# The first w2 of the second expert layer kept outside the ring

## The chip, the cores and the metric

The kernel runs on one core of one Trainium2 chip. The metric is the device time of one execution in microseconds (us). The kernel before took 1134.48 us, the median of three runs (1131.81 to 1135.38). Everything is float32.

## The reference

Two layers work on 256 tokens of width 1024. Layer 0 mixes tokens by causal pooling, layer 1 by differential attention. After each mixer comes a hierarchical mixture of experts: a router gives each token two of 32 experts, and each expert has three matrices of 2 MB.

```python
def hier_moe(h, wg, bg, we, be, w1, w3, w2):
    ...
    def expert_block(args):
        xb, e = args
        a = jax.nn.silu(xb @ w1[e]) * (xb @ w3[e])
        return a @ w2[e]
    ...

def reference(...):
    for i in range(DEPTH):
        ...                                  # i = 0: pool_mixer, i = 1: diff_attention
        h = rms_norm(x, norm_ffn_g[i])
        x = x + hier_moe(h, moe_wg[i], moe_bg[i], moe_we[i], moe_be[i],
                         moe_w1[i], moe_w3[i], moe_w2[i])
    return rms_norm(x, final_g)
```

## The kernel before

All weights stream through `ring`, eight slots of 2 MB (16 KB in each of 128 partitions). The kernel walks all 32 experts of a layer in order, whichever tokens they got. In what follows the matrices of layer 1 are counted c = 0, 1, 2, ... in the order w1, w3, w2 of expert 0, then of expert 1, and so on (c = 95 is the last). Matrix c goes to slot c % 8. Experts are named e0 to e31.

SyncE alone issues the weight loads, in program order, and each load is preceded by a wait for what last read its slot. For layer 1 it issues c0 and c1 when attention is done with wv (`s_vp`), c2 to c5 when all queries and keys are computed (`s_q`, NH), and c6 and c7 when the output projection is done (`s_wo`). From c8 on, the function `stream` waits for the products that used the slot: a w1 or w3 slot is free when the gate products of its expert are done (`m_gu`), a w2 slot when its down products are done (`m_y`). So c8 and c9 wait for the gate products of e0, c10 for the down products of e0, c11 and c12 for the gate products of e1, c13 for the down products of e1.

TensorE does for each expert: gate and up products from the two ring slots (L457, function `expert`), one part of the gathering of the next group's tokens (L411), then, when VectorE has turned the activations (L1069, `actT`), the down products (L493). Both product steps do one block of 32 tokens, and a second block under `pe.If(count > SB)` only where the expert has more than 32 tokens. After four experts (a group) TensorE adds the outputs back to the tokens (L510, `scatter`, here too one or two blocks by a branch). `keep_clock` (L363) adds products that nobody reads. Eight experts are the body of a loop of four iterations. VectorE and ScalarE copy each expert's output (L1095, L799) into `y`, which is the tensor `hT` by another name. `hT` holds the transposed tokens that the router's products read (L389, which end with `s_lg`). `work` is a scratch tensor of 6144 columns that holds, in turn, the pooling's tensors, q, k and v of attention, and the experts' gathered tokens `xg` and activations `sg`, `act`, `actT`.

Of the kernel before, what the change touches and what calls it, by code (L numbers as in the profile page):

```python
# [23 lines left out]
S, D = 256, 1024  # L24
TH = S // P
KT = D // P
NH, HD = 8, 64
# [3 lines left out]
JT = F // P  # L31
SB = 32
NB = 2
CAP = SB * NB
PASSES = S // CAP
E4 = P // SB
GPB = 2
BODY = GPB * E4
# [56 lines left out]
def build(nc, x, norm_mix_g, norm_ffn_g, pool_w, pool_scale, wq, wk, wv, wo, lq1, lk1, lq2, lk2, subln_g,  # L95
          moe_wg, moe_bg, moe_we, moe_be, moe_w1, moe_w3, moe_w2, final_g, consts, out):
    with ExitStack() as ctx:
# [3 lines left out]
        def sem(name):  # L101
            return ctx.enter_context(nc.semaphore(name))
# [34 lines left out]
        junk_o = small[:, 800:1056].rearrange("p (t e) -> p t e", t=TH)  # L137
        rows = work2[:, 1280:1280 + D]
        ones_row = small[:, 832:832 + P]
        we_raw = work[:, 5632:6144].rearrange("p (l n) -> p l n", l=2)  # L140
        wg_raw = work2[:, 0:64].rearrange("p (l n) -> p l n", l=2)


        band = work[:, 0:len(WINDOWS) * BW]
        pw = work[:, 1536:1536 + 2048].rearrange("p (g c d) -> p g c d", g=4, c=2)
        mixT = work[:, 3584:3584 + 2048].rearrange("p (m s) -> p m s", m=KT)

        diag = work[:, 0:S].rearrange("p (t q) -> p t q", t=TH)
        qk = work[:, 0:4096].rearrange("p (m h s) -> p m h s", m=2, h=NH)
# [5 lines left out]


        xg = work[:, 0:4096].rearrange("p (u k b e s) -> p u k b e s", u=2, k=KT, b=NB, e=E4)
        sg = work[:, 4096:5120].rearrange("p (m b f) -> p m b f", m=4, b=NB)
        act = work[:, 5120:5376].rearrange("p (b f) -> p b f", b=NB)
        actT = work[:, 5376:5632].rearrange("p (b r) -> p b r", b=NB)  # L160
        y = hT.rearrange("p k s -> p (k s)").rearrange("p (b n) -> p b n", b=NB)
        onehot = work2[:, 0:1024].rearrange("p (u t b e s) -> p u t b e s", u=2, t=TH, b=NB, e=E4)
        gated = work2[:, 1024:1536].rearrange("p (t b e s) -> p t b e s", t=TH, b=NB, e=E4)
# [22 lines left out]
        gain_in, gcol_in = sem("gain_in"), sem("gcol_in")  # L186
        s_diag, s_rr = sem("s_diag"), sem("s_rr")
        s_out = sem("s_out")

        s_ssq = sem("s_ssq")  # L190
        s_root = sem("s_root")
# [42 lines left out]
        def chunk_parts(layer, e, j):  # L234
# [3 lines left out]
                return (moe_w1, moe_w3)[j][layer, e, :, :].rearrange("(p k) n -> p (k n)", k=KT)  # L238
            return moe_w2[layer, e, :, :].rearrange("(p j) n -> p (j n)", j=JT)

        def swapped(e):

            return (CPE * e) % RING == RING - 1
# [14 lines left out]
        @block.sync  # L258
        def _(sp):
            def load(slot, src, signal):  # L260
                dst = ring[:, slot, :]
                if len(src.shape) == 3:
                    dst = dst.rearrange("p (k n) -> p k n", k=src.shape[1])
                sp.dma_start(dst, src).then_inc(signal, 16)

            def row(dst, src):

                return sp.dma_start(dst, src.to_broadcast([P] + list(src.shape[1:])))

            for r, g in enumerate((norm_mix_g[0:1, :], pool_scale[0:1, :])):  # L270
                sp.dma_start(rows[32 * r:32 * r + 1, :], g).then_inc(s_rows, 16)
            for t in range(TH):
                sp.dma_start(x_sb[:, t, :], x[0, t * P:(t + 1) * P, :]).then_inc(s_x[t], 16)
            sp.dma_start(band, consts[:, C_BAND:C_ALL]).then_inc(s_band, 16)
            sp.dma_start(pw, pool_w[0].rearrange("g (c p) d -> p g c d", p=P)).then_inc(s_pw, 16)
            sp.dma_start(cst[:, :], consts[:, 0:C_BAND]).then_inc(s_c, 16)
            for i, g in enumerate((norm_mix_g[1, :], norm_ffn_g[0, :], norm_ffn_g[1, :])):
                sp.dma_start(gcol[:, i, :], g.rearrange("(p k) -> p k", k=KT)).then_inc(gcol_in, 16)
            sp.dma_start(wg_raw, moe_wg.rearrange("l (p k) n -> p l (k n)", k=KT)).then_inc(s_wraw, 16)
            sp.dma_start(we_raw, moe_we.rearrange("l (p k) n -> p l (k n)", k=KT)).then_inc(s_wraw, 16)  # L280
            for layer in range(2):
                row(rb[:, layer, 0:NG], moe_bg[layer:layer + 1, :]).then_inc(s_rb, 16)
                row(rb[:, layer, NG:NR], moe_be[layer:layer + 1, :]).then_inc(s_rb, 16)

            used = (main["gu"], main["gu"], main["y"])
            attn_used = ((s_vp, 2), (s_vp, 2), (s_q, NH), (s_q, NH), (s_q, NH), (s_q, NH), (s_wo, 4), (s_wo, 4))
            for layer in range(2):
                for c in range(RING):
                    if layer == 1:
                        sp.wait_ge(*attn_used[c])  # L290
                    load(c, chunk_parts(layer, c // CPE, c % CPE), loaded[c])
                steady = CPE * BODY

                def stream(it, c):

                    e, j = divmod(c - RING, CPE)
                    sp.wait_ge(used[j], it * BODY + (layer * NE + e + 1))
                    load(c % RING, chunk_parts(layer, it * BODY + c // CPE, c % CPE), loaded[c % RING])

                with sp.Fori(0, ITERS - 1) as it:  # L300
                    for c in range(RING, RING + steady):
                        stream(it, c)
                for c in range(RING, steady):
                    stream(ITERS - 1, c)

                fb = more[layer]
                sp.wait_ge(s_route, layer + 1)
                most = sp.value_load(cnt[0:1, NE + NGRP:NE + NGRP + 1], min_val=0, max_val=S)
                with sp.If(most > CAP):

                    sp.wait_ge(main["y"], NE * (layer + 1))
                    with sp.Fori(0, PASSES - 1) as m:
                        with sp.If(most > CAP * m + CAP):
                            with sp.Fori(0, NE) as e:
                                n = m * NE + e
                                for j in range(CPE):
                                    load(j, chunk_parts(layer, e, j), fb[f"wl{j}"])
                                sp.wait_ge(fb["y"], n + 1)
                                sp.sem_inc(fb["passed"], 1)
                if layer == 0:  # L320
                    for c in range(ACH):
                        e, j = divmod(CPE * NE - RING + c, CPE)
                        sp.wait_ge(used[j], e + 1)
                        load(c, attn_parts(c), loaded[c])
            for t in range(TH):
                sp.wait_ge(s_h, 2 + t + 1)
                sp.dma_start(out[0, t * P:(t + 1) * P, :], h_sb[:, t, :]).then_inc(s_out, 16)
            sp.wait_ge(s_out, 32)
# [20 lines left out]
        def _(pe):  # L349
# [83 lines left out]
                        gather(s_xg1[layer], 0, r, FIRST[r], slice(P, 2 * P))  # L433
                    pe.wait_ge(s_xg1c[layer], E4)

            def group(s, g, u, placed, rounds, fullest, tokens, chunk):


                def second_block(count, step):
# [6 lines left out]
                def expert(k):  # L446
# [38 lines left out]
                    if k > 0:  # L485
                        for half in ("yc_v", "yc_a"):
                            pe.wait_ge(s[half], n1 - 1)
                    w = ring[:, chunk(k, 2), :].rearrange("p (j n) -> p j n", j=JT)

                    def down(b, js):  # L490
                        for j in js:
                            for i in range(4):
                                mm = pe.matmul(y_ps[SB * i:SB * (i + 1), b, :], actT[:, b, SB * j:SB * (j + 1)],  # L493
                                               w[:, j, 256 * i:256 * (i + 1)], start=(j == 0 and b == 0),
                                               stop=(j == JT - 1), skip_group_check=True)
                        return mm

                    down(0, range(0, 3))
                    second_block(count, lambda: down(1, range(0, 4)))
                    down(0, range(3, 4)).then_inc(s["y"], 1)  # L500
                    if k == E4 - 2:
                        keep_clock(FILL_NEXT, 7)
                    if k == E4 - 1:
# [24 lines left out]
            def experts(layer):  # L528
                u0 = use_before(layer)
                pe.wait_ge(s_hn, 2 * (layer + 1))  # L530
                first_blocks(layer)
                with pe.Fori(0, ITERS) as it:
                    for gg in range(GPB):
                        g = it * GPB + (layer * NGRP + gg)

                        def fullest(gg=gg):
                            return pe.value_load(cnt[0:1, bass.ds(it * GPB + (NE + gg), 1)], min_val=0, max_val=S)

                        def tokens(k, gg=gg):
                            return pe.value_load(cnt[0:1, bass.ds(it * BODY + (gg * E4 + k), 1)], min_val=0, max_val=S)  # L540

                        def chunk(k, j, gg=gg):
                            c = CPE * (gg * E4 + k) + j
                            pe.wait_ge(loaded[c % RING], (it * (CPE * BODY // RING) + (u0 + c // RING + 1)) * 16)
                            return c % RING

                        group(main, g, gg % 2, it * GPB + (layer * (NGRP + 1) + gg + 1),
                              it * (GPB * E4) + (layer * (NGRP + 1) + gg + 1) * E4, fullest, tokens, chunk)

            def passes(layer, most):  # L550
                fb = more[layer]
# [183 lines left out]
        def _(act_e):  # L735
# [172 lines left out]
                    copy_output(h - 4)  # L908
            for t in range(TH):
                copy_hT(2, t)  # L910
                norm(3, t, work[:, 4096:4096 + D])
                normalise_tokens(1, t)
            route(1)
            experts(1)
# [358 lines left out]
```

## Time and profile before

| | before |
|---|---|
| median of three runs | 1134.48 us |
| the profiled execution: device time | 1131.81 us |
| its span, first to last instruction | 1130.0 us |
| mean granted TensorE clock | 0.928 |
| TensorE busy | 880.1 us, 78% |
| VectorE busy | 345.5 us, 31% |
| ScalarE busy | 232.5 us, 21% |
| weight loads of the experts | 192 of 2048 KB |
| DMA moved | 427.19 MB, mean 378 GB/s |

The span is what the trace covers; the device time of the same execution has 1.81 us more around it. Times in the rows are microseconds from the span's start. A busy share is a mean over the whole span: it doesn't say which engine is waited for in a stretch.

### The profile page before, as it was taken

What the parts mean: (1) busy time and instruction counts of PE and PEld (TensorE: products, weight loads), DVE (VectorE), ACT (ScalarE), POOL (GpSimd) and SP (SyncE); (2) the same over time, 40 slices, a digit from 0 to 9 for tenths busy, and PEclk for the clock granted to TensorE, in tenths of its full rate; (3) what the DMA queues carried; (4) which work ended last, traced back from release to release, by engine and by line L of the source; (5) the groups of instructions that cost most, each with busy time, mean ns of one, the idle gap of its engine ahead of it and who ended that gap; (6) DMA issues with size and microseconds to landing.
All of it is one profiled execution on the core that took longest, in us unless ns stands there. A gap on an engine that the chain in (4) does not pass through costs nothing.

```text
span 1130.0 us, 19738 instructions
## 1 busy us (share of the span) xinstructions
PE 880.1 (78%) x8032; PEld 511.3 (45%) x8033; DVE 345.5 (31%) x821; ACT 232.5 (21%) x559; POOL 4.6 (0%) x14
## 2 busy tenths in 40 slices
PE   6878777677786778589999988787887676768766
PEld 5644434333443344344886554443544343334433
DVE  2523222321322223222366253231332222213314
ACT  2421111110211111112144322110221121102112
POOL 1000000000000000000000000000000000000000
PEclk9899989998998989899999999999998898989979
DMA  9999999999999999998405459999999999999992
GB/s 299 428 424 424 425 426 425 423 427 425 426 425 426 425 426 426 425 425 358 176 1 200 166 208 426 425 426 413 426 426 425 425 426 425 428 423 425 427 426 112
DMA packets 33478, 427.19 MB, mean 378 GB/s; under 512 B 4706, under 2 KB 5986, under 8 KB 7988
## 3 DMA queue, kind: packets, MB, share of 16 engines
q1 hardware_dynamic: 33028, 424.19, 89.2%
q8 instruction: 132, 2.16, 0.8%
q0 software_dynamic: 304, 0.72, 0.4%
q14 instruction: 14, 0.11, 0.0%
HBM read 423.85 MB, written 1.05 MB: 376 GB/s over the span
## 4 chain that ended last, share of the span: by engine, by line
DMA 44%; PE 41%; DVE 7%; issue 5%; ACT 2%; DVEq 0%; SPq 0%
DMA ring<-in_moe_w 43%; PE ps L457 14%; PE ps L493 6%; PE ps L631 5%; PE ps L510 3%; PE ps L613 2%; DVE work L1061 2%; PE ps L411 2%; PE ps L685 2%; PE ps L363 1%; DMA work<-in_consts 1%; DVE work L1069 1%; ACT work L791 1%; PE ps L389 1%; DVE work L1063 1%
## 5 line engine op out<-in xcount | busy, mean ns | idle before, releaser
L457 PE MATMUL ps<-ring,work 128*32 128x256 f32 x4224 | 298.2, 434 | 164.8 <-DMA ring<-in_moe_w 100.7
L457 PEld LDWEIGHTS ps<-ring,work 128*32 128x32 f32 x4224 | 165.8, 124 | 304.7 <-issue 210.0
L1059 DVE TENSOR_SCALAR work<-work 128x128 f32<-128x128 f32 (+1 forms) x64 | 14.6, 229 | 501.3 <-ACT work L791 501.3
L493 PE MATMUL ps<-ring,work 128*32 128x256 f32 x2112 | 127.5, 382 | 30.8 <-DVE work L1069 30.2
L411 PE MATMUL ps<-work,h_sb 128*128 128x256 f32 (+1 forms) x576 | 136.2, 380 | 4.5 <-issue 3.8
L1095 DVE COPY hT<-ps 32x512 f32<-32x512 f32 x128 | 87.4, 683 | 149.0 <-PE ps L493 148.1
L791 ACT ACTIVATE work<-ps 128x256 f32<-128x256 f32 x64 | 24.5, 383 | 510.2 <-PE ps L457 510.2
L411 PEld LDWEIGHTS ps<-work,h_sb 128*128 128x128 f32 x576 | 99.6, 190 | 42.8 <-issue 32.9
L493 PEld LDWEIGHTS ps<-ring,work 128*32 128x32 f32 x2112 | 62.9, 109 | 92.9 <-DVE work L1069 44.9
L799 ACT COPY hT<-ps 32x512 f32<-32x512 f32 x128 | 73.9, 577 | 123.6 <-PE ps L493 122.9
L764 ACT ACTIVATE work<-ps,gcol 128x256 f32<-128x256 f32 (+1 forms) x144 | 58.6, 458 | 110.7 <-PE ps L411 110.7
L363 PE MATMUL ps<-cst,small 128*128 128x512 f32 x160 | 79.8, 613 | 0.0
L510 PE MATMUL ps<-hT,work 128*128 128x512 f32 x136 | 62.6, 604 | 11.1 <-DVE hT L1095 11.1
L1061 DVE RECIPROCAL work<-work 128x128 f32<-128x128 f32 (+1 forms) x64 | 62.6, 978 | 2.2
L631 PE MATMUL ps<-hT,ring 128*128 128x256 f32 x256 | 56.5, 380 | 0.0
L631 PEld LDWEIGHTS ps<-hT,ring 128*128 128x128 f32 x256 | 48.1, 190 | 6.6 <-DVE work L1189 0.3
L510 PEld LDWEIGHTS ps<-hT,work 128*128 128x128 f32 x136 | 24.5, 189 | 49.2 <-issue 49.2
L363 PEld LDWEIGHTS ps<-cst,small 128*128 128x128 f32 x160 | 27.8, 189 | 29.3 <-issue 28.5
L685 PE MATMUL ps<-ring,work 128*128 128x512 f32 x64 | 28.6, 594 | 0.0
L613 PE MATMUL ps<-ring,hT 128*128 128x512 f32 x64 | 27.9, 593 | 0.8 <-DVE hT L953 0.8
L1069 DVE STREAM_TRANSPOSE work<-work 128x128 f32<-128x128 f32 x66 | 26.5, 404 | 2.2
L481 PE MATMUL ps<-cst,work 128*128 128x128 f32 x64 | 10.5, 286 | 14.9 <-ACT work L764 14.9
(146 smaller groups left out, 420.8 us busy)
## 6 DMA issues: line engine op xcount, KB each, us to landing
ring<-in_moe_w SPq DMA_DIRECT2D x192, 2048.0 KB, 30.4
ring<-in_attn_wv SPq DMA_DIRECT2D x2, 2048.0 KB, 33.0
ring<-in_attn_wq SPq DMA_DIRECT2D x2, 2048.0 KB, 32.0
ring<-in_attn_wk SPq DMA_DIRECT2D x2, 2048.0 KB, 34.0
ring<-in_attn_wo SPq DMA_DIRECT2D x2, 2048.0 KB, 37.1
x_sb<-in_x SPq DMA_DIRECT2D x2, 512.0 KB, 5.7
work<-in_pool_w SPq DMA_DIRECT2D x1, 1024.0 KB, 13.0
out_x<-h_sb SPq DMA_DIRECT2D x2, 512.0 KB, 2.6
```

The source lines that it names most:

```text
L363: pe.matmul(ps[:, bank, :], zero, cst[:, 0:512], start=True, stop=True)
L411: mm = pe.matmul(xg_ps(bank)[:, q, cols], h_sb[:, t, kt * P:(kt + 1) * P], onehot[:, u, t].rearrange("p b e s -> p (b e s)")[:, cols], sta ...
L457: mm = pe.matmul(gu_ps[SB * j:SB * (j + 1), b, :, :], xg[:, u, kt, b, k, :], w[:, :, kt, P * j:P * (j + 1)], start=(kt == 0 and b == 0), s ...
L493: mm = pe.matmul(y_ps[SB * i:SB * (i + 1), b, :], actT[:, b, SB * j:SB * (j + 1)], w[:, j, 256 * i:256 * (i + 1)], start=(j == 0 and b == ...
L510: mm = pe.matmul(acc[:, t, i, :], gateT[:, b, t * P:(t + 1) * P], y[:, b, 512 * i:512 * (i + 1)], start=False, stop=False, skip_group_chec ...
L613: mm = pe.matmul(ps[:, 2 * t + i, :], hT[:, kt, t * P:(t + 1) * P], matrix(0, kt)[:, 512 * i:512 * (i + 1)], start=(kt == 0), stop=(kt == ...
L631: mm = pe.matmul(ps[:, h % 2, i * S:(i + 1) * S], matrix(2 + 2 * i, kt)[:, h * P:(h + 1) * P], hT[:, kt, :], start=(kt == 0), stop=(kt == ...
L685: mm = pe.matmul(ps[:, 2 * t + i, :], qT[:, h, t * P:(t + 1) * P], matrix(6, h)[:, 512 * i:512 * (i + 1)], start=(h == 0), stop=(h == NH - 1))
L764: ins = act_e.mul(xg[:, u, kt].rearrange("p b e s -> p (b e s)")[:, cols], xg_ps(bank)[:, q, cols], gcol[:, 1 + layer, kt:kt + 1])
L799: ins = act_e.copy(y[SB * k:SB * (k + 1), :, 256 * i:256 * (i + 1)], y_ps[SB * i:SB * (i + 1), :, :])
L1061: ve.reciprocal(sg[:, 2, b, :], sg[:, 1, b, :]).then_inc(s["sig"], 1)
L1095: ins = ve.tensor_copy(y[SB * k:SB * (k + 1), :, 256 * i:256 * (i + 1)], y_ps[SB * i:SB * (i + 1), :, :])
```

## The change

The w2 of layer 1's e0 (c2) no longer goes to ring slot 2. It is loaded in two halves of 1 MB (8 KB in each partition) to two places outside the ring: `work[:, 2560:4608]`, once the last head's attention is done (`s_o`), and `hT`, once the router's products are done (`s_lg`). Slot 2 takes c10, the w3 of e3, at the point where c2 was loaded. In the first iteration of the loop `stream` passes over c10. TensorE reads e0's w2 from the two places in the first iteration and from slot 2 in the others, so the down products of the loop's first expert stand twice in the code, behind a branch. Since slot 2 has had one load less, its readers wait for a count that is one lower. In `work` the activations move up by 512 columns, so that columns 2560 to 4608 lie free until the second expert's gathering writes there.

```diff
-        we_raw = work[:, 5632:6144].rearrange("p (l n) -> p l n", l=2)
+        we_raw = work[:, 3584:4096].rearrange("p (l n) -> p l n", l=2)
...
-        mixT = work[:, 3584:3584 + 2048].rearrange("p (m s) -> p m s", m=KT)
+        mixT = work[:, 4096:4096 + 2048].rearrange("p (m s) -> p m s", m=KT)
...
-        sg = work[:, 4096:5120].rearrange("p (m b f) -> p m b f", m=4, b=NB)
-        act = work[:, 5120:5376].rearrange("p (b f) -> p b f", b=NB)
-        actT = work[:, 5376:5632].rearrange("p (b r) -> p b r", b=NB)
+        sg = work[:, 4608:5632].rearrange("p (m b f) -> p m b f", m=4, b=NB)
+        act = work[:, 5632:5888].rearrange("p (b f) -> p b f", b=NB)
+        actT = work[:, 5888:6144].rearrange("p (b r) -> p b r", b=NB)
+        aside = (hT.rearrange("p k s -> p (k s)"), work[:, 2560:4608])
...
+        EARLY_C, ASIDE_C = RING + CPE - 1, CPE - 1
...
+            w2_aside = chunk_parts(1, 0, CPE - 1)
             for layer in range(2):
-                for c in range(RING):
+                for slot in range(RING):
+                    if layer == 1 and slot == RING - 2:
+                        sp.wait_ge(s_o, NH)
+                        sp.dma_start(aside[1], w2_aside[:, 2048:4096]).then_inc(s_aside, 16)
                     if layer == 1:
-                        sp.wait_ge(*attn_used[c])
-                    load(c, chunk_parts(layer, c // CPE, c % CPE), loaded[c])
+                        sp.wait_ge(*attn_used[slot])
+
+                    c = EARLY_C if layer == 1 and slot == ASIDE_C else slot
+                    load(slot, chunk_parts(layer, c // CPE, c % CPE), loaded[slot])
+                if layer == 1:
+                    sp.wait_ge(s_lg, 2)
+                    sp.dma_start(aside[0], w2_aside[:, 0:2048]).then_inc(s_aside, 16)
...
                     for c in range(RING, RING + steady):
-                        stream(it, c)
+                        if layer == 1 and c == EARLY_C:
+                            with sp.If(it > 0):
+                                stream(it, c)
+                        else:
+                            stream(it, c)
...
+                    def outputs(w):
+                        down(w, 0, range(0, 3))
+                        second_block(count, lambda: down(w, 1, range(0, 4)))
+                        down(w, 0, range(3, 4)).then_inc(s["y"], 1)
+
+                    def from_ring():
+                        slot = chunk(k, 2)
+                        outputs((ring[:, slot, 0:2048], ring[:, slot, 2048:4096]))
+
+                    if first is not None and k == 0:
+                        with pe.If(first > 0):
+                            from_ring()
+                        with pe.Else():
+                            pe.wait_ge(s_aside, 32)
+                            outputs(aside)
+                    else:
+                        from_ring()
...
+                            ahead = 1 if layer == 1 and c % RING == ASIDE_C else 0
+                            pe.wait_ge(loaded[c % RING], (it * (CPE * BODY // RING) + (u0 + c // RING + 1 - ahead)) * 16)
...
-                norm(3, t, work[:, 4096:4096 + D])
+                norm(3, t, work[:, 4608:4608 + D])
```

SyncE, from the loads that fill the ring for layer 1 to the first loads of the loop, before:

```order
L264 DMA ring<-in_moe_w 128x4096 [waits s_q] x4
L264 DMA ring<-in_moe_w 128x4096 [waits s_wo] x2
L300 UNCONDITIONAL_BRANCH
L300 ISA
L264 ISA [waits m_gu]
L264 DMA ring<-in_moe_w 128x4096
L264 ISA [waits m_gu]
L264 DMA ring<-in_moe_w 128x4096
L264 DMA ring<-in_moe_w 128x4096 [waits m_y]
L297 REGISTER_ALU
L264 DMA ring<-in_moe_w 128x4096 [waits m_gu]
```

And the same place of the changed kernel:

```order
L270 DMA ring<-in_moe_w 128x4096 [waits s_q] x4
L298 DMA work<-in_moe_w 128x2048 [waits s_o]
L270 DMA ring<-in_moe_w 128x4096 [waits s_wo] x2
L306 DMA hT<-in_moe_w 128x2048 [waits s_lg]
L315 UNCONDITIONAL_BRANCH
L315 ISA
L270 ISA [waits m_gu]
L270 DMA ring<-in_moe_w 128x4096
L270 ISA [waits m_gu]
L270 DMA ring<-in_moe_w 128x4096
L318 COMPARE_AND_BRANCH
L270 DMA ring<-in_moe_w 128x4096 [waits m_y]
```

Two half loads stand ahead of the loop, one before and one behind the loads c6 and c7, and the load of c10 is now behind a branch.

TensorE, the down products of the first expert of layer 1's loop body (e0, e8, e16, e24), before:

```order
L411 MATMUL ps<-work,h_sb 128x256 x3
L484 ISA
L493 MATMUL ps<-ring,work 32x256 [waits loaded2,m_actT]
L493 MATMUL ps<-ring,work 32x256 x11
L443 COMPARE_AND_BRANCH
L493 MATMUL ps<-ring,work 32x256 x16
L443 UNCONDITIONAL_BRANCH
L493 MATMUL ps<-ring,work 32x256 x4
L540 ISA
```

And of the changed kernel:

```order
L503 ISA
L526 COMPARE_AND_BRANCH [waits m_actT]
L578 ISA
L511 MATMUL ps<-ring,work 32x256 [waits loaded2]
L511 MATMUL ps<-ring,work 32x256 x11
L462 COMPARE_AND_BRANCH
L511 MATMUL ps<-ring,work 32x256 x16
L462 UNCONDITIONAL_BRANCH
L511 MATMUL ps<-ring,work 32x256 x4
L526 UNCONDITIONAL_BRANCH
L511 MATMUL ps<-hT,work 32x256 [waits s_aside]
L511 MATMUL ps<-hT,work 32x256 x7
```

The wait for the activations now stands on a branch. In the first iteration it jumps over 32 products to the copy that reads `hT` and `work`; in the others it falls through and a jump at the end passes over that copy.

## Rows read from the trace of the kernel before

**Rows 1.** Page, the span in 40 slices of 28 us: clock, DMA, GB/s.

```profile
PEclk9899989998998989899999999999998898989979
DMA  9999999999999999998405459999999999999992
GB/s 299 428 424 424 425 426 425 423 427 425 426 425 426 425 426 426 425 425 358 176 1 200 166 208 426 425 426 413 426 426 425 425 426 425 428 423 425 427 426 112
```

**Rows 2.** Busy time by stretch; the last three columns are clock, DMA share, GB/s.

```profile
560.00:606.00 46.00, 46.00 (x253) 38.66 (x252) 28.25 (x91) 16.54 (x72) 0.00 (x0) 1.00 0.00 1
629.00:644.00 15.00, 15.00 (x47) 7.39 (x45) 2.22 (x4) 2.85 (x9) 0.00 (x0) 1.00 0.00 0
644.00:656.00 12.00, 9.89 (x42) 7.09 (x41) 6.62 (x28) 7.39 (x12) 0.00 (x0) 0.72 0.89 350
656.00:668.00 12.00, 10.34 (x109) 7.51 (x110) 5.33 (x24) 2.90 (x10) 0.00 (x0) 1.00 0.01 3
668.00:1111.00 443.00, 337.53 (x3572) 184.12 (x3574) 122.06 (x247) 78.14 (x163) 0.00 (x0) 0.93 0.99 419
```

**Rows 3.** Timeline of SyncE, its load issues: start, length, line, how many.

```profile
643.59 0.80 SPq L264 DMA_DIRECT2D ring<-in_moe_w  x2
...
667.97 0.90 SPq L264 DMA_DIRECT2D ring<-in_moe_w  x2
...
676.01 5.71 SPq L264 DMA_DIRECT2D ring<-in_moe_w  x3
...
787.52 0.88 SPq L264 DMA_DIRECT2D ring<-in_moe_w  x2
```

**Rows 4.** Issues by size, us to landing: those at 606.46, 643.59, 766.24, 787.52.

```profile
ring<-in_moe_w SPq DMA_DIRECT2D x1, 2048.0 KB, 8.9
...
ring<-in_moe_w SPq DMA_DIRECT2D x1, 2048.0 KB, 7.8
...
ring<-in_moe_w SPq DMA_DIRECT2D x1, 2048.0 KB, 24.7
...
ring<-in_moe_w SPq DMA_DIRECT2D x1, 2048.0 KB, 8.4
```

**Rows 5.** Timeline of TensorE: start, length, line, tile, count, idle time before.

```profile
624.67 0.39 PE L668 MATMUL ps<-work 128*128 128x128 f32 x2
...
648.21 3.60 PE L389 MATMUL ps<-wr,hT 128*128 128x36 f32 x16 [0.87 <-DVE hT L953]
...
716.09 2.79 PE L457 MATMUL ps<-ring,work 128*32 128x256 f32 x47 [0.25 <-DMA ring<-in_moe_w]
...
724.72 2.15 PE L493 MATMUL ps<-ring,work 128*32 128x256 f32 x32
730.95 9.38 PE L457 MATMUL ps<-ring,work 128*32 128x256 f32 x124 [4.08 <-DMA ring<-in_moe_w]
...
1108.52 3.66 PE L457 MATMUL ps<-ring,work 128*32 128x256 f32 x64 [0.93 <-DMA ring<-in_moe_w]
```

**Rows 6.** Chain that ended last, 655 to 835 us: start, length, what.

```profile
670.11 0.42 DVE work L1069
670.57 1.93 PE ps L493 x32
...
702.09 28.73 DMA ring<-in_moe_w
730.95 9.64 PE ps L457 x128
...
751.23 7.09 PE ps L457 x128
...
776.08 4.29 issue
...
823.34 0.29 issue
```

**Rows 7.** Busy time by stretch, as rows 2, while TensorE's clock was halved.

```profile
731.00:736.00 5.00, 5.00 (x48) 2.68 (x52) 0.00 (x0) 0.00 (x0) 0.00 (x0) 0.50 1.02 429
```

More of the change, by code:

```diff
@@ L188, in build @@
         s_out = sem("s_out")
+        s_aside = sem("s_aside")
         s_ssq = sem("s_ssq")
@@ L434, in first_blocks, with group @@
                     pe.wait_ge(s_xg1c[layer], E4)
-            def group(s, g, u, placed, rounds, fullest, tokens, chunk):
+            def group(s, g, u, placed, rounds, fullest, tokens, chunk, first=None):
                 def second_block(count, step):
@@ L487, in expert, with down @@
                             pe.wait_ge(s[half], n1 - 1)
-                    w = ring[:, chunk(k, 2), :].rearrange("p (j n) -> p j n", j=JT)
-                    def down(b, js):
+                    def down(w, b, js):
                         for j in js:
+                            wj = w[j // 2][:, D * (j % 2):D * (j % 2 + 1)]
                             for i in range(4):
                                 mm = pe.matmul(y_ps[SB * i:SB * (i + 1), b, :], actT[:, b, SB * j:SB * (j + 1)],
-                                               w[:, j, 256 * i:256 * (i + 1)], start=(j == 0 and b == 0),
+                                               wj[:, 256 * i:256 * (i + 1)], start=(j == 0 and b == 0),
                                                stop=(j == JT - 1), skip_group_check=True)
                         return mm
-                    down(0, range(0, 3))
-                    second_block(count, lambda: down(1, range(0, 4)))
-                    down(0, range(3, 4)).then_inc(s["y"], 1)
+                    def outputs(w):
[13 more added lines that the diff above has]
+                        from_ring()
                     if k == E4 - 2:
@@ L543, in chunk @@
                             c = CPE * (gg * E4 + k) + j
-                            pe.wait_ge(loaded[c % RING], (it * (CPE * BODY // RING) + (u0 + c // RING + 1)) * 16)
+                            ahead = 1 if layer == 1 and c % RING == ASIDE_C else 0
+                            pe.wait_ge(loaded[c % RING], (it * (CPE * BODY // RING) + (u0 + c // RING + 1 - ahead)) * 16)
                             return c % RING
                         group(main, g, gg % 2, it * GPB + (layer * (NGRP + 1) + gg + 1),
-                              it * (GPB * E4) + (layer * (NGRP + 1) + gg + 1) * E4, fullest, tokens, chunk)
+                              it * (GPB * E4) + (layer * (NGRP + 1) + gg + 1) * E4, fullest, tokens, chunk,
+                              it if layer == 1 and gg == 0 else None)
             def passes(layer, most):
```

## The prediction

> **What bounds the kernel now.** I began with the slices of the page [rows 1]. The DMA row stands at 9 nearly everywhere, with some 425 GB/s, and has one hole, in slices 19 to 24: attention and the second routing. Outside the hole the loads set the pace; in the hole something else does. So the question is how much of the hole can be filled, and whether a load taken out behind it shortens the end.
>
> The busy times by stretch give the hole's parts [rows 2]. From 560 to 606 us the queue moves nothing (share 0.00), since all slots are taken. From 629 to 644 us again nothing. From 644 to 656 us c6 and c7 move (350 GB/s). From 656 to 668 us nothing (0.01), because the ring is full and e0's gate products are not yet done. From 668 to 1111 us the share is 0.99 without a break, at 419 GB/s. In that stretch lie c8 to c95, 88 loads: at 2.097 MB each, 184.5 MB, which at 419 GB/s take 440 of the 443 us. One load costs there 2.097 / 0.419 = 5.0 us. At the end e31's gate products wait for the queue (start 1108.52, 0.93 us idle for a load) [rows 5]. So layer 1's end hangs on the queue from 668 us on.
>
> Then I asked at which point the queue itself depends on TensorE. A load issued with nothing ahead of it lands after 7.8 to 8.9 us; in the middle of the stream it takes far longer, since it queues: the one at 766.24 took 24.7 us, so it landed at 790.9. The next one, c32 at 787.52, took 8.4 us [rows 3, 4]: it landed at 795.9, 5.0 us behind its forerunner, just in step. Its slot came free only then, with the gate products of e8. So at this one point the queue had run almost dry, and a queue that is 5 us further on would find it dry. The chain of waits [rows 6] shows what sets that point: a load (28.73 us from 702.09) that ends at e6's gate products at 730.95, and from there TensorE and what it needs, to e8.
>
> **The change, part by part.**
>
> *One load leaves the stream.* c10 is no longer issued behind c9; c11 follows c9. Gain 5.0 us, if c11 is there in time. c8 and c9 are issued at 667.97, c11 at 676.01 [rows 3]. Two loads at 5.0 us, behind a start like the one at 643.59 (7.8 us to landing) [rows 4], bring c9 down at about 667.97 + 7.8 + 5.0 = 680.8, and c11 would be due at 685.8; issued at 676.01 and with 7.8 to 8.9 us unqueued it could land at 684.9 at the latest. It is not late. From there two of three issues come with a gate step and one with a down step, and the queue only gets longer until e5.
>
> *c10 takes c2's place*, issued at about 607 us in the same order: nothing. *The half in `work`* waits for the last head (L668 ends at 625.1) [rows 5], long before the wait of c6 at 643.59 [rows 3], so it holds nothing up; 1 MB takes 2.5 us and moves in the empty stretch 629 to 644 [rows 2]. Were that cover gone, it would cost its 2.5 us. *The half in `hT`* waits for the router's products (648.21 + 3.60 = 651.8) [rows 5]. It stands behind c6 and c7 in the queue, which move until 656 [rows 2], so its 2.5 us end at 658.5; with the 2 us or so that landings lie behind the data (7.8 less the 5.0 of the transfer is 2.8 for both ends) it is there by 661.5. e0's down products start at 670.57 [rows 6]: 9 us to spare. Behind this wait on SyncE stands the loop's first load, which isn't wanted before 667.97. Nothing.
>
> *The branch in e0.* Down products that follow a plain wait start 0.04 us behind VectorE's transpose (670.11 + 0.42 to 670.57). Where TensorE waits and then takes a jump to the Else part, as in `scatter`, the same gap is 0.29 us (the piece "issue" at 823.34) [rows 6]. So the new jump costs 0.25 us if its target is at hand. The upper bound is the jump back at the loop's end, 4.29 us of "issue" [rows 6]. The new jump is forward and over 32 products, double the 16 that the existing ones skip; it is nearer the first, and I take 0.25. The jump at the end of the Else part and in the later iterations lies behind queued products or while TensorE waits for loads: nothing.
>
> The Trainium skill speaks against this jump ("Runtime: NRT & Kernel Launch", Instruction fetch mechanics): instructions come in pages of 16 KiB, only two are held, and a taken branch whose target lies outside them stalls until the page is fetched. By it the sum would be 0.25 us or the stall's full length; no row shows that length for a forward jump by itself.
>
> *What becomes of the point at 787.52.* In the chain e5 starts at 716.09 after 0.25 us of waiting for a load, ends its down products at 726.87, and e6 waits 4.08 us for its w3, which lands at 702.09 + 28.73 = 730.82 [rows 5, 6]. Five us earlier that load lands at 725.8. So e6 starts when e5 is done: 726.87 - 0.25 (its own wait is gone) + 0.25 (the jump) = 726.9, 4.05 us earlier. There is more. In that wait the granted clock fell: 0.50 from 731 to 736, the lower of its two levels (1.2 instead of 2.4 GHz) [rows 7]. e6's gate step took 9.64 us, e7's, of the same 128 products, 7.09 [rows 6]. Without the wait e6 should take 7.1 too, 2.55 us less. The gate products of e8 would then be done 6.6 us earlier and c32 issued at 780.9. It is due to land at 795.9 - 5.0 = 790.9, so it has 10 us, and needs 7.8 to 8.9. The queue doesn't run dry, and the 5.0 us are kept. Behind it the chain returns to loads, and everything to the end moves with the queue.
>
> **Sum.** -5.0 us of stream, 0 for the halves, 0 for the jump (it eats into slack). Span 1130.0 - 5.0 = 1125.0 us; with the 1.81 us around it 1126.8 us. The profiled execution was the shortest of the three, 2.67 us below the median, so against the median I say 1134.48 - 5.0 = 1129.5 us.
>
> **The rivals.**
>
> 1. *The clock isn't won back* (10 in 100). If some other idle piece halves the clock before e8, e6's 2.55 us stay. c32 is then issued at 783.5 and lands 7.8 to 8.9 us later, 791.3 to 792.4 instead of 790.9: 0.4 to 1.5 us lost. Gain 3.5 to 4.6, time 1129.9 to 1131.0. For it: the clock also fell elsewhere in this layer [rows 1]. Against: no wait of that size is left between e0 and e8 but the loop's jump, which is there before as well.
>
> 2. *The new jump stalls TensorE* (12 in 100). Price up to the 4.29 us of the loop's jump, with a halved clock behind it up to 6.8. c11 is then issued at 680.3 and lands at 688.1 at the earliest, 2.3 us late. e6 starts at 726.6 + 4.3 = 730.9, without the low clock before it, or with it at 733.5: c32 is issued between 785.0 and 787.5 and the gain is 2.5 down to 0. Time 1132.0 to 1134.5. The Trainium skill's page rule would make this the outcome. So far the trace is half for it: short jumps in scatter cost 0.29, the long one back 4.29.
>
> 3. *Slower: the doubled code makes TensorE stall twice in the first iteration* (5 in 100), at the jump in and at the one out, each at the 4.29 us of the only long jump, with one halved clock behind. e6 would start at about 735.2, its clock won back or not, and c32 be issued at about 790 to 792 instead of 787.52: the queue runs dry for 2.5 to 4.5 us, time 1137 to 1139. It decides when TensorE loses more than 6.6 us between e0 and e8 (4.05 of wait and 2.55 of clock).
>
> 4. *The load isn't really taken out* (5 in 100): the early loads push c6 and c7 back, or the queue is held elsewhere. If both halves lay in the way that is 5.0 us, gain 0, 1134.5. Against it speak the empty stretches.
>
> **How the numbers follow.** The forecast has 68 in 100, own range 1128.2 to 1130.8. A measurement of this kernel tells about 0.3%, 3.4 us, from no change. The forecast and most of rival 1 lie beyond it, a part of them falls within by scatter of the medians (three runs spread over 3.6 us): faster 0.76. Rivals 2 and 4 with that part: same 0.19. Rival 3: slower 0.05. The range reaches down by scatter to 1127.0 and up into rival 2, to 1132.8.
>
> **What would show it.** Right: two half loads, at about 625 and 652 us; the queue without a break from 668 us on and its end about 5 us earlier; e6 starting at about 727 with hardly any wait and a gate step of about 7.1 us; the load behind e8's gate products issued near 781 and landing after more than 9 us; 0.3 us between VectorE's transpose and e0's down products. Wrong: a gap of several us there; a DMA share below 0.99 around 680 or 790 us; e6's gate step still near 9.6 us; e31 no longer waiting for its loads.

## The result: no gain, 0.18% slower

The changed kernel took 1134.88 us (median of 20 runs, 1132.82 to 1138.89), the kernel before 1132.72 us (median of 20, 1130.77 to 1135.38). The ratio is 1.0018, 95% interval 1.0011 to 1.0026. Forecast were 1129.5 us and a gain of 5.0. Over 20 runs the kernel before is 1.76 us below the median of three that stood ahead of the prediction. The profiled execution of the changed kernel is its longest, 1138.89 us with a span of 1137.1. It is 7.1 us longer than the profiled one before, where the medians are 2.2 us apart, so what the trace loses below is more than the median does.

The slices of the page, as in [rows 1]. The queue is short of work at two places where it was not before: at the end of the hole (slice 25, 381 GB/s instead of 426), and in slices 28 and 29, 768 to 825 us (360 and 406 instead of 413 and 426):

```profile
PEclk9899989888998989899999889998899889989988
DMA  9999999999999999998306559998999999999992
GB/s 299 424 426 424 428 421 428 424 429 421 428 424 429 422 427 424 428 422 335 151 1 251 203 214 381 424 425 360 406 426 424 428 424 426 425 425 424 427 424 97
```

Busy time by stretch, columns as in [rows 2]. The stretch 629 to 644 us, empty before, now carries one half (share 0.13). The stretch from 668 us, which had a share of 0.99 as a whole before, has 0.67 up to 684 (e3 below has 0.94 there):

```profile
629.00:644.00 15.00, 15.00 (x45) 7.26 (x43) 2.07 (x3) 2.41 (x7) 0.00 (x0) 1.00 0.13 55
...
668.00:684.00 16.00, 9.92 (x107) 5.25 (x108) 3.52 (x7) 2.66 (x6) 0.00 (x0) 0.89 0.67 265
...
686.00:1116.00 430.00, 329.99 (x3444) 178.35 (x3448) 116.81 (x237) 75.35 (x157) 0.00 (x0) 0.92 0.99 416
```

SyncE's issues, as in [rows 3]. Both halves go out where they were meant to (625.62 and 652.72), c8 and c9 at 668.54. But c11 goes out at 683.72, 15.2 us behind c8, where it was 8.0 before, and c32 at 792.20:

```profile
625.62 0.33 SPq L298 DMA_DIRECT2D work<-in_moe_w  x1
...
652.72 0.33 SPq L306 DMA_DIRECT2D hT<-in_moe_w  x1
...
668.54 0.89 SPq L270 DMA_DIRECT2D ring<-in_moe_w  x2
...
683.72 1.17 SPq L270 DMA_DIRECT2D ring<-in_moe_w  x2
...
792.20 0.87 SPq L270 DMA_DIRECT2D ring<-in_moe_w  x2
```

Their sizes and times to landing, as in [rows 4]: the two halves, then c11 and c32. c11 landed at 691.3 and c32 at 801.2, each like a load with nothing ahead of it:

```profile
work<-in_moe_w SPq DMA_DIRECT2D x1, 1024.0 KB, 7.3
...
hT<-in_moe_w SPq DMA_DIRECT2D x1, 1024.0 KB, 7.7
...
ring<-in_moe_w SPq DMA_DIRECT2D x1, 2048.0 KB, 7.6
...
ring<-in_moe_w SPq DMA_DIRECT2D x1, 2048.0 KB, 9.0
```

TensorE's timeline shows why, against [rows 5]. L511 are the down products, L476 the gate products:

```profile
671.51 1.07 PE L511 MATMUL ps<-hT,work 128*32 128x256 f32 x16 [1.26 <-DVE work L1104]
672.40 0.61 PE L511 MATMUL ps<-work 128*32 128x256 f32 x8
677.68 0.79 PE L511 MATMUL ps<-work 128*32 128x256 f32 x8 [4.67 <-issue]
678.63 5.03 PE L476 MATMUL ps<-ring,work 128*32 128x256 f32 x64 [0.16 <-issue]
...
732.77 3.62 PE L476 MATMUL ps<-ring,work 128*32 128x256 f32 x59
737.42 4.08 PE L476 MATMUL ps<-ring,work 128*32 128x256 f32 x69 [1.03 <-issue]
...
745.74 5.35 PE L511 MATMUL ps<-ring,work 128*32 128x256 f32 x64 [2.31 <-DVE work L1104]
...
779.81 0.40 PE L476 MATMUL ps<-ring,work 128*32 128x256 f32 x1 [2.25 <-issue]
784.68 4.91 PE L476 MATMUL ps<-ring,work 128*32 128x256 f32 x62 [4.47 <-issue]
791.60 0.40 PE L476 MATMUL ps<-ring,work 128*32 128x256 f32 x1 [2.02 <-issue]
...
802.07 6.44 PE L476 MATMUL ps<-ring,work 128*32 128x256 f32 x64 [5.12 <-issue]
...
1113.89 5.35 PE L476 MATMUL ps<-ring,work 128*32 128x256 f32 x64 [3.10 <-DMA ring<-in_moe_w]
```

There are five things to see. The jump into the Else part itself is cheap: 1.26 us of wait, where 0.88 to 1.07 stand at this place in the kernels that don't jump behind the wait. In the Else part, at the skip of the second block, TensorE stands still for 4.67 us ("issue": nothing in the profile that it waits for), and then works at the lower level of its clock for a while (granted 0.66 in the mean from 677 to 682 us), so that e1's gate products take 5.03 us instead of the 3.64 that stand in e3 below. Behind the first copy, which e8 uses, it stands still for 5.12 us: that is the jump over the Else part, and the same jump takes as long behind e16 and e24. At the jump back of the loop, ahead of and in e8's gate products, the idle pieces are 2.25, 4.47 and 2.02 us, where they were 0.77, 4.29 and 1.21 before. And e6's down products take 5.35 us instead of 3.66, at the lower level of the clock.

The trace has a record of the branch itself. This is the skip of the second block in e0's down products (shortest, median and longest in ns; here there is one):

```profile
L462 PEldq COMPARE_BRANCH  x1: 6010/6010/6010, 671.6 to 671.6; - x1
```

The same skip took 219 ns in the kernel before, and the next one, in e1's gate products, 342 ns.

Where the load stream stood still: c9 landed at 669.09 + 12.9 = 682.0, c11 at 691.3, 9.3 us later instead of 5.0, so 4.3 us are lost. c31 landed at 768.87 + 24.6 = 793.4, c32 at 801.2, 7.8 us later, so 2.8 are lost. Together that is 7.1 us against the 5.0 gained, a loss of 2.1, near the 2.2 between the medians. But the profiled execution lost more: its last load landed 5.4 us later than before (1118.6 against 1113.3). c9 had landed 0.4 us later there, and from c11 to c31 it took 2.8 us longer (102.1 against 99.4 us). What lengthened this stretch was not tried. Another 1.7 us lie behind the last load, in e31's gate products (5.35 us at 1113.89, 3.66 before).

### The profile page after: what moved, and what is told of

Read it like the earlier page. It is cut to its first block, busy times and chain, and to the rows that moved or that the text cites. A ratio compares the mean times of both kernels' runs of the same rounds, so it can differ in the third digit from the quotient of the medians.

```text
span 1137.1 us, 19747 instructions
## 1 busy us (share of the span) xinstructions
PE 890.1 (78%) x8032; PEld 514.6 (45%) x8033; DVE 345.8 (30%) x821; ACT 232.9 (20%) x559; POOL 4.6 (0%) x14
## 4 chain that ended last, share of the span: by engine, by line
PE 46%; DMA 35%; DVE 8%; issue 8%; ACT 2%; DVEq 0%; SPq 0%
DMA ring<-in_moe_w 34%; PE ps L476 17%; PE ps L511 7%; PE ps L666 5%; PE ps L542 4%; DVE work L1096 3%; PE ps L648 2%; PE ps L430 2%; PE ps L720 2%; PE ps L382 1%; DVE work L1104 1%; ACT work L826 1%; DMA work<-in_consts 1%; PE ps L413 1%; PE ps L408 1%
## 5 line engine op out<-in xcount | busy, mean ns | idle before, releaser
L476 PE MATMUL ps<-ring,work 128*32 128x256 f32 x4224 | 303.2, 442 | 156.4 <-DMA ring<-in_moe_w 79.8
L476 PEld LDWEIGHTS ps<-ring,work 128*32 128x32 f32 x4224 | 167.2, 126 | 298.7 <-issue 208.8
L1094 DVE TENSOR_SCALAR work<-work 128x128 f32<-128x128 f32 (+1 forms) x64 | 14.7, 230 | 497.9 <-ACT work L826 497.9
L511 PE MATMUL ps<-ring,work 128*32 128x256 f32 x2080 | 129.1, 386 | 32.7 <-DVE work L1104 30.8
L826 ACT ACTIVATE work<-ps 128x256 f32<-128x256 f32 x64 | 24.6, 384 | 506.6 <-PE ps L476 506.6
L511 PEld LDWEIGHTS ps<-ring,work 128*32 128x32 f32 x2080 | 63.3, 110 | 96.6 <-DVE work L1104 41.2
```

The costliest lines, as they stand in the source:

```text
L476: mm = pe.matmul(gu_ps[SB * j:SB * (j + 1), b, :, :], xg[:, u, kt, b, k, :], w[:, :, kt, P * j:P * (j + 1)], start=(kt == 0 and b == 0), s ...
```

## The experiments

All ratios are to the kernel before, run beside them on the same chip (medians 1132.2 us for e1 to e4, 1132.4 for e5 to e8). e1 and e5 leave something out: their loop's first expert reads the places aside in every iteration, so the w2 of e8, e16 and e24 are loaded but not used.

### e1: the change without branch and second copy

```diff
-                        with pe.If(first > 0):
-                            from_ring()
-                        with pe.Else():
-                            pe.wait_ge(s_aside, 32)
-                            outputs(aside)
+                        chunk(k, 2)
+                        pe.wait_ge(s_aside, 32)
+                        outputs(aside)
```

> The change with its branch and its second copy of the down products taken out: the loop's first expert always reads its w2 from the two places aside. Left out: the w2 of e8, e16 and e24 of layer 1 are loaded but not used. Theory (the instructions skipped in the first iteration lie on a page that isn't there, TensorE stalls 4.7 us at e0 and the load stream breaks): no idle piece of over 1.5 us in e0's down products, c11 issued near 676 instead of 683.7, the stream without a gap of over 0.5 us there, about 5 us faster than before (ratio 0.995 to 0.997). Rival (the early load itself gives nothing, or the two half loads disturb the routing): within 0.15% of before.

Measured: 1132.95 us, ratio 1.0005 (0.9996 to 1.0014). The stall in the down products is gone, but the gain did not come. So my theory of the doubled code was not the whole. The profiled execution is one of e1's shortest (1130.51 us). In it c11 is in time again (it landed 5.7 us behind c9), but c32, issued at 786.70, landed 8.0 us behind c31, so 3.0 us were lost there. TensorE's timeline of e1 has a new idle piece, in the gate products of the second expert:

```profile
670.83 1.07 PE L511 MATMUL ps<-hT,work 128*32 128x256 f32 x16 [1.07 <-DVE work L1102]
671.69 1.07 PE L511 MATMUL ps<-work 128*32 128x256 f32 x16
672.55 1.94 PE L476 MATMUL ps<-ring,work 128*32 128x256 f32 x32
677.30 1.93 PE L476 MATMUL ps<-ring,work 128*32 128x256 f32 x32 [2.81 <-issue]
```

### e2: only branch and second copy, no load moved

```diff
...
+                    def outputs():
+                        down(0, range(0, 3))
+                        second_block(count, lambda: down(1, range(0, 4)))
+                        down(0, range(3, 4)).then_inc(s["y"], 1)
+
+                    if first is not None and k == 0:
+                        with pe.If(first > 0):
+                            outputs()
+                        with pe.Else():
+                            outputs()
+                    else:
+                        outputs()
...
```

> The kernel before with only the branch and the second copy of the down products, both copies reading the ring; no load is moved. Theory: TensorE has the same stall of 4 to 6 us at e0 and after the first down products of each later iteration; c32 is issued some 4 us later than before and the queue runs dry there by about as much, so 3 to 6 us slower than before (ratio 1.003 to 1.005). Rival (the stall belongs to the new tiles or the wait for them, not to the code): the same time as before and no stall at e0.

Measured: 1135.16 us (7 runs), ratio 1.0033 (1.0021 to 1.0045). The stall is there without the new tiles, at the same two places (timeline of e2, e0's down products and e9's gate products):

```profile
675.98 0.88 PE L493 MATMUL ps<-ring,work 128*32 128x256 f32 x8 [4.15 <-issue]
...
799.49 4.71 PE L457 MATMUL ps<-ring,work 128*32 128x256 f32 x56 [5.41 <-issue]
```

So the code of the change costs 0.33% by itself, and by the difference to the change (1.0018) the moved load was worth some 0.15% beside it, with intervals that overlap.

### e3: the change, first iteration written out on TensorE

```diff
-                    if first is not None and k == 0:
-                        with pe.If(first > 0):
-                            from_ring()
-                        with pe.Else():
-                            pe.wait_ge(s_aside, 32)
-                            outputs(aside)
+                    if isinstance(first, int) and k == 0:
+                        pe.wait_ge(s_aside, 32)
+                        outputs(aside)
...
-                with pe.Fori(0, ITERS) as it:
+                def body(it):
                     for gg in range(GPB):
...
+                if layer == 1:
+                    body(0)
+                    with pe.Fori(1, ITERS) as it:
+                        body(it)
+                else:
+                    with pe.Fori(0, ITERS) as it:
+                        body(it)
```

In `body(0)` the down products of e0 read the places aside, with no branch.

> The change with TensorE's first iteration of layer 1 written out ahead of the loop (the loop has three iterations then), so that no branch is needed to choose the copy. Theory: no stall at e0, and the jump back ahead of e8 with its 4.3 us is gone too, so the queue has more slack at c32: 5 us faster than before (ratio 0.995 to 0.997), the same as or a little better than the kernel without a branch. Rival (more code means more stalls elsewhere, or the gain is given back at c32): within 0.15% of before, with the load behind e8's gate products landing later than its forerunner plus 6 us.

Measured: 1127.58 us (5 runs, 1126.74 to 1128.68), ratio 0.996 (0.9948 to 0.9973). This version beats both kernels, and the profile has what the prediction wanted. Timeline of TensorE: no idle piece in e0 or at the start of e1, e6 at 726.99 in 7.11 us, and e8 at 768.40 with no stall ahead of it:

```profile
671.66 1.05 PE L511 MATMUL ps<-work 128*32 128x256 f32 x16
672.52 3.64 PE L476 MATMUL ps<-ring,work 128*32 128x256 f32 x64
...
726.99 7.11 PE L476 MATMUL ps<-ring,work 128*32 128x256 f32 x128
...
738.34 3.66 PE L511 MATMUL ps<-ring,work 128*32 128x256 f32 x64 [2.32 <-DVE work L1109]
...
768.40 3.66 PE L476 MATMUL ps<-ring,work 128*32 128x256 f32 x64
```

Busy time by stretch: the stream has the share and rate of [rows 2] (0.99 and 419 GB/s), over 438 us instead of 443. Its last load landed at 1107.8 us, before at 1113.3:

```profile
668.00:1106.00 438.00, 335.36 (x3580) 183.03 (x3580) 122.11 (x247) 78.34 (x163) 0.00 (x0) 0.95 0.99 419
```

### e4: the kernel before, first iteration written out

The same edit as in e3 to the kernel before; no load is moved.

> The kernel before with TensorE's first iteration of layer 1 written out ahead of the loop; no load is moved. Theory: the loads set the pace through layer 1 and there is no gap in their stream at c32 before, so TensorE's 4.3 us at the jump back gain next to nothing: ratio 0.999 to 1.001, and the whole gain of the peeled change belongs to the moved load. Rival (the jump back before e8 costs the queue something already): 1 to 4 us faster, ratio 0.997 to 0.999.

Measured: 1131.5 us, ratio 0.9993 (0.9984 to 1.0002). Writing the iteration out gains next to nothing alone; the moved load gains 1131.5 - 1127.6 = 3.9 us on top of it. What the missing jump back gives to the moved load can't be told apart in these two, since e4 has no load moved; e5 and e6 below keep the loop.

### What e1 left open

In e1 nothing jumps that did not jump before, yet a stall of 2.81 us stands in e1's gate products, which the kernel before hasn't got. The order of the instructions gave a second theory. (The sequencer is the part of TensorE that takes the instructions one by one; branches and register instructions are its own work.) In the kernel before, the wait for the activations sits on the first down product: it is held there, and the sequencer has already passed the instructions ahead of it. In e1 a register had to be set for a count of its own between that wait and the products, and the wait sits on that register instruction; in the change it sits on the branch. In both the sequencer itself holds the wait. The idle piece of e1 sits on a jump too, but an old one, the skip of the second block in e1's gate products. That branch took 4237 ns, in the kernel before 342:

```profile
L462 PEldq COMPARE_BRANCH  x2: 337/2287/4237, 670.9 to 673.0; - x2
```

### e5: e1 with the wait put back on the product

The edit, against e1:

```diff
+                    apart = first is not None and k == 0
+                    if apart:
+                        chunk(k, 2)
+                        pe.wait_ge(s_aside, 32)
                     pe.wait_ge(s["actT"], n1)
...
-                    if first is not None and k == 0:
-                        chunk(k, 2)
-                        pe.wait_ge(s_aside, 32)
+                    if apart:
                         outputs(aside)
```

> The kernel of e1 with one thing moved: the waits for the two halves and the ring slot now come before the wait for the activations, so that this last wait rides on the first down product and not on a register instruction of TensorE's sequencer. Left out as in e1: the w2 of e8, e16 and e24. Theory (a wait held by the sequencer keeps it from reaching the next page of instructions while it waits, and the page is then fetched late, beside the load stream): the idle piece of 2.8 us in e1's gate products is gone or below 0.5 us, c11 issued near 676, and the moved load is worth 3 to 5 us (ratio 0.995 to 0.998). Rival (e1's idle pieces come from where the code lies, whatever holds the wait): the same pieces and the same time as e1, ratio 0.9995 to 1.0014.

Measured: 1128.6 us (5 runs), ratio 0.9963 (0.995 to 0.9977). The trace has as many instructions as e1's (19745), in another order, and the median is 4.3 us less than e1's; all five runs lie below all eleven of e1. The two profiled executions are only 0.4 us apart (1130.11 and 1130.51), the longest of e5 and one of the shortest of e1, so the traces show the idle piece going away but only a part of the 4.3 us. At c32 the queue was still nearly dry: c32 went out at 787.01, took 8.3 us, and landed 6.7 us behind c31, so 1.7 us were lost there. Its timeline, against e1's rows (it entered the layer 2 us later):

```profile
672.70 1.07 PE L515 MATMUL ps<-hT,work 128*32 128x256 f32 x16 [0.88 <-DVE work L1104]
673.58 1.05 PE L515 MATMUL ps<-work 128*32 128x256 f32 x16
674.45 3.64 PE L476 MATMUL ps<-ring,work 128*32 128x256 f32 x64
```

### e6: the change with its branch ahead of the wait

```diff
-                    pe.wait_ge(s["actT"], n1)
+                    apart = first is not None and k == 0
+                    if not apart:
+                        pe.wait_ge(s["actT"], n1)
...
-                    if first is not None and k == 0:
+                    if apart:
                         with pe.If(first > 0):
-                            from_ring()
+                            slot = chunk(k, 2)
+                            pe.wait_ge(s["actT"], n1)
+                            outputs((ring[:, slot, 0:2048], ring[:, slot, 2048:4096]))
                         with pe.Else():
                             pe.wait_ge(s_aside, 32)
+                            pe.wait_ge(s["actT"], n1)
                             outputs(aside)
```

> The change with its branch put before the wait for the activations (each copy waits for them by itself), nothing left out. Theory: the 3 us of that wait cover the jump and the fetch of the page behind it, e0's stall of 4.7 us falls below 1.5 us, and the kernel is 2 to 5 us faster than before (ratio 0.996 to 0.998). Rival (the doubled code costs a page more however it is waited for): a stall of 4 us or more stays in e0 or e1 and the ratio is 1.000 to 1.002.

Measured: 1129.62 us, ratio 0.9977 (0.9968 to 0.9986), faster than before, with nothing left out and the loop as it was. The down products of e0 run through; an idle piece of 2.29 us is left in e1's gate products (timeline of e6). My bound of 1.5 us was for e0's stall; I had not expected a piece in e1:

```profile
672.38 3.23 PE L476 MATMUL ps<-ring,work 128*32 128x256 f32 x56
677.90 0.64 PE L476 MATMUL ps<-ring,work 128*32 128x256 f32 x8 [2.29 <-issue]
```

### e7: the kernel before, with the wait held by the sequencer

```diff
                     pe.wait_ge(s["actT"], n1)
...
+                    if k == 0 and late is not None:
+                        pe.wait_ge(loaded[2], late)
...
```

`late` is a count of the ring slot that was long reached, but needs a register of its own.

> The kernel before with a needless register instruction and wait between the wait for e0's activations (and e8's, e16's, e24's) and its down products, so that the sequencer holds the wait. Nothing else is changed. Theory: an idle piece of 2 to 4 us appears in e1's gate products, e2 starts 2 to 4 us later than before, and since the load stream isn't further on here, the time changes little: ratio 0.999 to 1.001. Rival (who holds the wait doesn't matter): no such piece.

Measured: 1133.72 us, ratio 1.0011 (1.0002 to 1.002), just above what was expected. The piece is there in its timeline, and its branch took 4310 ns:

```profile
672.41 1.94 PE L457 MATMUL ps<-ring,work 128*32 128x256 f32 x32
677.23 1.93 PE L457 MATMUL ps<-ring,work 128*32 128x256 f32 x32 [2.88 <-issue]
```

The DMA queues show what the hold delays. From 667.5 to 670.4 us, while e0's activations are made, the kernel before moves one packet of instructions beside the loads (packets, MB, share of the 16 engines):

```profile
q1 hardware_dynamic: 20, 0.33, 53.8%
q8 instruction: 1, 0.02, 2.1%
```

e7 moves none in that stretch. Its packet comes after it, from 670.4 to 676 us, between 159 packets of weights:

```profile
q1 hardware_dynamic: 159, 2.34, 98.3%
q8 instruction: 1, 0.02, 1.1%
```

All ten traces agree on the packet. Where the sequencer held the wait, in the change, e1, e2 and e7, the first packet of instructions behind 667 us starts at 673.6 to 675.3 us. In the other six it starts at 668.3 to 669.1 (671.0 in e5, which entered the layer 2 us later). In six traces TensorE has an idle piece of 1.41 to 4.67 us in e0's down or e1's gate products (the change, e1, e2, e6, e7, e8; in e6 and e8 behind a second packet). In each of them the products go on 1.40 to 1.47 us after the end of an instruction packet. So these pieces are waits for instructions.

### e8: e2 with its branch ahead of the wait

The edit of e6, to e2's kernel: each copy waits for the activations by itself.

> The kernel of e2 (before, with the branch and the second copy, no load moved) with its branch put before the wait for the activations. Theory: the stall of 4.1 us in e0's down products falls below 1.5 us and most of e2's loss of 0.33% goes: ratio 0.999 to 1.002. Rival (the second copy costs a page fetch in each iteration, wherever the branch stands): ratio 1.002 to 1.005.

Measured: 1134.58 us, ratio 1.002 (1.0011 to 1.0029). The stall in the down products is gone (1.41 us are left in e1's gate products), but much of the loss stays, and 1.002 is the border between what I and what the rival expected. In its trace, 2.7 us longer than the one before, c32 was issued at 791.23, behind the loop's jump back, and landed 7.2 us behind c31, so 2.2 us were lost there. Its interval and e2's overlap, so how much of the 0.33% goes back to the wait is not settled.

## Why the prediction was wrong, by its own steps

**One load leaves the stream, -5.0 us: right in size.** With TensorE undisturbed the stream is 5 us shorter (e3: 438 against 443 us at the same rate), and 3.9 us of it are left in the medians (e3 against e4).

**The two halves cost nothing: right.** They moved in the empty stretches, landed at 632.9 and 660.4, and e0's down products, at 671.51, waited for the activations.

**The branch in e0, 0.25 us: the step that failed.** The jump in was cheap, as priced. What I had not asked is what the next instructions behind it need. I took the 0.29 us of `scatter` as the nearest row, but there the jump passes over 8 products. Here a skip of 32 products and one of 16 follow each other, and the place stalled for 4.67 us, close to the upper bound of 4.29 that I had from the jump back and had set aside. "The jump at the end of the Else part [...] nothing" failed too: the jump over it in the later iterations took 5.12 us (e9), 5.41 in e2. e2 shows that both come from the code alone. Rival 2 was the likeliest of the rivals and had the mechanism. That its time of 1132.0 to 1134.5 lies near the 1134.88 measured is in part luck, since the kernel before came out 1.76 us lower over 20 runs. As a difference it said a gain of 2.5 to 0, and 2.2 were lost. Rival 3 had a second stall and c32 issued at 790 to 792, which is where it was (792.20), but put the second stall in the first iteration; it came in the second, behind c32. Their chances of 12 and 5 in 100 were too low: I had a bound of 4.3 us that nothing excluded and let the cheaper row decide.

The Trainium skill's rule ("Runtime: NRT & Kernel Launch", Instruction fetch mechanics), that a taken branch out of the two pages held stalls until its page is fetched, fits both stalls. Which page held which instruction no row shows. e1 and e7 show something that the rule doesn't say: an old jump, which took 0.34 us before, took 4.24 and 4.31 us when the wait ahead was held by the sequencer.

**c11 is not late: failed with it.** It was due at 685.8 by my sum and landed at 691.3, because e1's gate products, which free its slot, ended late: it went out at 683.72 instead of 676.01 [rows 3]. The slack I found, 0.9 us, was below any stall.

**The point at 787.52: right as a place, wrong in its slack.** I had 1.6 us over: c32 issued at 780.9. It was issued at 792.20, 4.7 us later than before instead of 6.6 earlier. Some 2.1 of these 4.7 us came at the loop's jump back, which the prediction left as it was: from the end of the products that add e4's to e7's outputs to the tokens to the issue of c32 it took 14.7 us (777.55 to 792.20), before 12.6 (774.92 to 787.52). The first idle piece there is 2.11 to 2.35 us in the four kernels with the doubled code in the loop (the change, e2, e6, e8), and 0.48 to 0.78 in the others that keep the loop. The stalls took TensorE's wait for e6's load (4.08 us before, none now), as rival 2 says. The clock gained less than 2.55 us. In the change e6's gate products took 8.7 us (732.77 to 741.50, with 1.03 us idle) instead of 9.64, but its down products took 5.35, where the chain of the kernel before has 3.66 for them (from 744.80). In e3, where e6 starts at 726.99, both steps are short (7.11 and 3.66), and the 2.55 us are there in full. So rival 1 was right in part too: the clock can fall a step later. For the 790.9 of my sum c32 would have had to go out by about 783; in e3 it went out at 772.29 and took 19.7 us to land.

**Behind c32 everything moves with the queue: right.** From c32 to the last load it took 317.4 us (801.2 to 1118.6), before 317.3 (795.9 to 1113.3), and e31's gate products still wait for a load (3.10 us, at 1113.89). So what the queue had lost by c32 went to the end.

## What to carry to other kernels

Price a branch by the code that it adds and makes the sequencer pass, not by the jump alone: here, with the weight stream full, TensorE stood still for 2.8 to 5.4 us where its instructions came late. Keep the long wait of a step on the engine's own instruction (set registers and take the cheap waits first). In e5 and e6, which do that, the packet of instructions set out before the activations were there. When a load is taken out of a stream that bounds the kernel, look for each point where the queue is nearly dry: the gain is only kept if the slots come free by the gain earlier there too.

## What the hardware showed that I had not expected

- The order of the waits was worth 4.3 us in the medians: e1 against e5, 1132.95 and 1128.6 us, with as many instructions. e7 makes the same stall (2.88 us) in the kernel before, with one register instruction and one wait more.
- That the packet of instructions comes while the activations are made (before) or after it (e7) is shown. When it is asked for has no record. In the change, e1 and e7 it starts 4.2 to 4.4 us after the sequencer is let go; that it is slow because it stands among the weight packets is inferred, from its place between 159 of them.
- TensorE's granted clock fell from 2.4 to 1.2 GHz after a wait of only 2.31 us for the activations, ahead of e6's down products. Busy time by stretch, change first, then e3, where the engine had waited 2.32 us just the same and the clock stayed:

```profile
746.40:749.60 3.20, 3.20 (x36) 1.64 (x32) 0.00 (x0) 0.00 (x0) 0.00 (x0) 0.50 1.00 425
```

```profile
742.00:746.00 4.00, 4.00 (x31) 1.80 (x34) 1.37 (x2) 1.15 (x2) 0.00 (x0) 1.00 0.97 414
```

All ten traces have this wait, of 2.30 to 2.33 us. The clock fell behind it in seven (the products took 5.35 us) and stayed in three (3.66 us): in the kernel before, e3 and e6. What decides was not tried.
